# Bringing the first scale and shift in the order of the rows, ahead of a three-tile first projection

## The reference, cut to what matters

```python
def modulate(h, shift, scale):
    return h * (1 + scale) + shift

# trunk_layer, its beginning
sh1, sc1, gt1, sh2, sc2, gt2 = [m[:, None, :] for m in adaln_params(c, w_ada, b_ada)]   # silu(c) @ w_ada + b_ada, split in 6
shc1, scc1, gtc1, shc2, scc2, gtc2 = adaln_params(c_ctx, w_ada, b_ada)
h = modulate(rmsnorm(x, g1), sh1, sc1)
hc = modulate(rmsnorm(xc, g1), shc1, scc1)
z = h @ w_in                     # w_in: 1024 x 2304, here 18 tiles of 128 columns
```

## Time and profile before

| What | before |
|---|---|
| median of 3 runs | 2249.05 us (2247.86, 2249.05, 2258.78) |
| the profiled execution's own time | 2259.43 us |
| its span | 2257.6 us |
| mean granted TensorE clock | 0.978 |
| PE busy | 2152.4 us, 95% |
| DVE, ACT, POOL busy | 58%, 48%, 21% |
| DMA | 355.01 MB, mean 157 GB/s |

### The profile page before, as it was taken

One profiled execution on the slowest core, in us unless ns is written; L12 is line 12 of the kernel. 1 busy time (PEld: TensorE's weight loads), 2 busy tenths in 40 slices (PEclk: granted clock), 3 DMA queues, 4 the chain that ended last, 5 costly groups with the idle time before them and its releaser, 6 DMA issues.

```text
span 2257.6 us, 44527 instructions
## 1 busy us (share of the span) xinstructions
PE 2152.4 (95%) x19132; PEld 2028.1 (90%) x19132; DVE 1298.6 (58%) x2521; ACT 1088.5 (48%) x1880; POOL 479.4 (21%) x226
## 2 busy tenths in 40 slices
PE   4999999999999999998899998999999999999998
PEld 3977999999998789998778888999999999999998
DVE  2355454343344667565673456498388896666665
ACT  2443353232235446445442445555577776555554
POOL 0200100000002220001111342088856662000000
PEclk8999999999999999999899999999999999999999
DMA  7224333444444445764233325466544445555553
GB/s 282 76 103 150 127 117 134 162 154 168 169 160 144 139 165 183 243 205 137 98 131 113 131 85 187 140 208 186 187 131 143 149 148 173 186 187 187 186 187 129
DMA packets 97284, 355.01 MB, mean 157 GB/s; under 512 B 10688, under 2 KB 11712, under 8 KB 96704
## 3 DMA queue, kind: packets, MB, share of 16 engines
q1 hardware_dynamic: 97088, 352.18, 46.7%
HBM read 351.09 MB, written 1.05 MB: 156 GB/s over the span
## 4 chain that ended last, share of the span: by engine, by line
PE 85%; DVE 5%; ACT 3%; DMA 3%; issue 2%; POOL 2%; SPq 0%; ACTq 0%; DVEq 0%; POOLq 0%
PE ps L79 79%; PE ps L84 4%; DVE TL L114 2%; ACT TH L158 2%; PE ps L107 1%; DMA RAW<-in_wada 1%; POOL TL L114 1%; DMA RAW<-in_wdn 1%; ACT SQ L155 1%; DMA RAW<-in_wup 1%; POOL SM L114 0%; ACT Hh L158 0%; DVE ps L114 0%; DMA RAW<-in_win 0%; DVE SQ L114 0%
## 5 line engine op out<-in xcount | busy, mean ns | idle before, releaser
L158 ACT ACTIVATE TH<-RAW 128x1024 fp32r<-128x1024 f32 (+1 forms) x515 | 539.9, 1049 | 429.1 <-PE ps L79 197.9
L114 DVE TENSOR_TENSOR TL<-RAW,TH 128x1024 fp32r<-128x1024 f32 (+1 forms) x343 | 421.0, 1228 | 477.8 <-ACT TH L158 477.3
L114 POOL TENSOR_TENSOR TL<-RAW,TH 128x1024 fp32r<-128x1024 f32 x172 | 414.0, 2410 | 522.3 <-ACT TH L158 496.0
L79 PE MATMUL ps<-Hh,TL 128*128 128x256 f32 x1920 | 450.5, 287 | 24.5 <-ACT Hh L158 14.1
L79 PE MATMUL ps<-Hh,TH 128*128 128x256 f32 x1920 | 439.0, 281 | 0.0
L79 PE MATMUL ps<-Hl,TH 128*128 128x256 f32 x1920 | 438.0, 280 | 0.0
L79 PE MATMUL ps<-HXh,TL 128*128 128x256 f32 x1312 | 366.4, 283 | 5.7 <-POOL TL L114 2.6
L79 PEld LDWEIGHTS ps<-Hh,TL 128*128 128x128 f32 x1920 | 321.7, 191 | 53.4 <-issue 32.7
L79 PE MATMUL ps<-W,TH 128*128 128x256 f32 x2048 | 361.9, 281 | 0.0
L79 PE MATMUL ps<-HXh,TH 128*128 128x256 f32 x1312 | 360.7, 279 | 0.0
L79 PE MATMUL ps<-HXl,TH 128*128 128x256 f32 x1312 | 360.5, 279 | 0.0
(11 more groups left out here) (323 smaller groups left out, 3006.1 us busy)
## 6 DMA issues: line engine op xcount, KB each, us to landing
RAW<-in_wada SPq DMA_DIRECT2D x144, 512.0 KB, 3.6
RAW<-in_ut SPq DMA_DIRECT2D x128, 512.0 KB, 3.5
RAW<-in_v SPq DMA_DIRECT2D x128, 512.0 KB, 3.7
RAW<-in_wup SPq DMA_DIRECT2D x88, 512.0 KB, 4.3
RAW<-in_win SPq DMA_DIRECT2D x74, 512.0 KB, 4.4
RAW<-in_wdn SPq DMA_DIRECT2D x32, 512.0 KB, 4.4
RAW<-in_wout SPq DMA_DIRECT2D x24, 512.0 KB, 3.6
RAW<-in_wq SPq DMA_DIRECT2D x16, 512.0 KB, 3.5
```

The source lines that it names most:

```text
L79: return self.e.matmul(out, lhs, rhs, start=first, stop=last, skip_group_check=skip)
L114: return DRY if self.e is None else self.e.tensor_tensor(out, a, b, op)
L158: return DRY if self.e is None else self.e.activation(out, a, ACT.Copy, **kw)
```

## The change

What it does, in order of the program:

- Group 1 of w_ada now fetches the columns of group 2 and the other way round (`ADA_PLACE`), so that the first 8 tiles give shift and scale of rows 0 to 3, the next 8 those of rows 4 to 7.
- ("head", 0) has 6 tiles and ("head", 1) two; the other 8 are at ("side", 1) to ("side", 4), two each. In the list they lie behind w_in tiles 0, 1 and 2.
- DVE adds the squares of all 8 rows, so that `norm` on PE has 4 pieces instead of 16. `spread` follows ("head", 1). The lam products, their Exp and their four small DVE operations go to the very front.
- `scales` for this norm becomes `first_scales(0)`, after `columns(1)`, and `first_scales(1)`, after `columns(3)` in the middle of `norm_rows`. ACT makes rows 0 to 3, and before row 4 runs ("side", 1) to ("side", 4) and waits for the second half.
- w_in tile 0's low is made by DVE, tile 1's and 2's by POOL; ACT splits tiles 0 and 1 before the rows, tile 2 before row 2.
- `project_side` takes w_in tiles 0, 1 and 2. Rows 0 to 3 run on tiles 0 and 1, with two tiles of w_ada in front of each of rows 1, 2, 3 and 4; in front of row 4 also `columns(3)`, and then tile 2's rows 0 to 3. Row 4 runs on all three, rows 5 to 7 tile by tile.
- The constants go out in front of tile 24 instead of 18.

```diff
@@ weight_tiles
-            add(("wada", b, i), ins[f"wada{b}"][i], split=False)
+            add(("wada", b, i), ins[f"wada{b}"][4 * (ada_place(12 * b + i // 4) - 12 * b) + i % 4], split=False)
...
-        for i in WIN_FIRST[l]:
-            add(("win", l, i), win[i], pool=2)
+        for z, i in enumerate(WIN_FIRST[l]):
+            add(("win", l, i), win[i], pool=2 if l or z > 2 else min(z, 1))
+            if l == 0 and z == 2:
+                for k in range(1, 5):
+                    ada("side", k)
@@ _ada_plan
-    plan = [(("head", 0), 8), (("head", 1), 8)]
+    plan = [(("head", 0), 6), (("head", 1), 2)] + [(("side", k), 2) for k in range(1, 5)]
...
-ADA_TURNED = (3, 9, 35)
+ADA_TURNED = (1, 3, 9, 35)
+ADA_PLACE = {1: 2, 2: 1}
+def ada_place(g):
+    return ADA_PLACE.get(g, g)
@@ tensor_program, norm
-            pe.wait_ge(D if tag == ("n1", 0) else G, "sum", *tag, 4)
-            for k in range(4, 8):
-                if k > 4:
+            added = added_of(tag)
+            pe.wait_ge(D if tag == ("n1", 0) else G, "sum", *tag, added)
+            for k in range(added, 8):
+                if k > added:
                     pe.wait_ge(A, "square", *tag, k)
@@ project_side
             for n in range(together):
-                if n == 4 and midway:
-                    midway()
-                for z in range(len(tiles)):
+                if midway:
+                    midway(n)
+                if behind and n == behind:
+                    split_done(tiles[-1])
+                    for k in range(behind):
+                        row(len(tiles) - 1, k)
+                for z in range(len(tiles) - (n < behind)):
                     row(z, n)
@@ tensor_program, the head
-        ada("head", 0)
-        norm(("n1", 0), 512)
-        spread(("n1", 0), ROOT[0][:, 0:4], 1, D, "h_norm", "m1", 0, 7)
         for l in range(DEPTH):
             pe.wait_ge(D, "lp", l)
             o = bank(("lam", l), A, "le", l)
             pe.mm(o[:, 0:2], ones[0:32, :], nlam_lp[l][0:32, :], True, True).then_inc(*P.mark("lam", l))
+        ada("head", 0)
+        norm(("n1", 0), 512)
         ada("head", 1)
-        columns(3)
+        spread(("n1", 0), ROOT[0][:, 0:4], 1, D, "h_norm", "m1", 0, 7)
+        columns(1)
+        def side(n):
+            ada("side", n)
+            if n == 4:
+                columns(3)
...
-                project_side([("win", l, 0), ("win", l, 1)], h(T), T, h1, (A, "u", l, 0), (A, "u", l, 1))
-                for j in range(2):
-                    win(2 + j, T, A, "tr", l, "va", j)
+                project_side([("win", l, i) for i in range(3)], h(T), T, h1, (A, "u", l, 0), (A, "u", l, 1),
+                             (A, "tr", l, "va", 0), together=5, midway=side, behind=4)
+                win(3, T, A, "tr", l, "va", 1)
@@ add_squares
+    def added_of(tag):
+        return 7 if tag == ("n1", 0) else 4
-        for k in range(1, 5):
+        for k in range(1, added_of(tag) + 1):
@@ scalar_program
         def ada(*point):
-                if point[0] != "gap":
+                if point[0] != "gap" and g > 3:
                     highs(at_tile["wada", b, i] + AHEAD)
         def high_rows(tag, l, slot, shift, t, dst, streams):
-            act.wait_ge(D, "scale", *tag)
-            act.wait_ge(D, "ada", 12 * l + 2 * shift + 1)
+            if tag == ("m1", 0):
+                act.wait_ge(D, "scale", *tag, 0)
+            else:
+                act.wait_ge(D, "scale", *tag)
+                act.wait_ge(D, "ada", 12 * l + 2 * shift + 1)
             for k in range(8):
+                if tag == ("m1", 0) and k == 2:
+                    highs(at_tile["win", 0, 2])
+                if tag == ("m1", 0) and k == 4:
+                    for n in range(1, 5):
+                        ada("side", n)
+                    act.wait_ge(D, "scale", *tag, 1)
...
+        for l in range(DEPTH):
+            act.wait_ge(P, "lam", l)
+            act.act(nlam_le[l], ps("lam", l)[:, 0:2], ACT.Exp).then_inc(*A.mark("le", l))
         act.wait_sem("x_in", s_x, 16)
...
         ada("head", 1)
+        highs(at_tile["win", 0, 1])
@@ vector_program
         def ada(*point):
-                if point[0] != "gap":
+                if point[0] != "gap" and 12 * b + i // 4 > 3:
                     lows(at_tile["wada", b, i] + AHEAD)
+        def first_scales(half):
+            c = slice(8 * half, 8 * half + 8)
+            o = MOD[:, c].rearrange("p (m c) -> p m c", c=2)
+            src = ADAS[0][:, 16 + 8 * half:24 + 8 * half].rearrange("p (m c) -> p m c", c=2)
+            dve.wait_ge(D, "ada", 1 + 2 * half)
+            dve.ts(o, src, 1.0, 32.0, ALU.add, ALU.mult).then_inc(*D.mark("scale1", "m1", 0, half))
+            dve.wait_ge(D, "scale1", "m1", 0, half)
+            dve.tt(o, o, par("n1g0", 4 * half, 4 * half + 4).rearrange("p (m o) -> p m o", o=1).to_broadcast([128, 4, 2]),
+                   ALU.mult).then_inc(*D.mark("scale", "m1", 0, half))
@@ norm_rows, behind X times the spread of row k
+                if tag == ("m1", 0) and k == 6:
+                    for n in range(1, 5):
+                        ada("side", n)
+                    columns(3)
+                    first_scales(1)
@@ vector_program, the head
         ada("head", 1)
-        columns(3)
-        scales(("m1", 0), 0, "n1g0", 1, 0)
+        lows(at_tile["win", 0, 0])
+        columns(1)
+        first_scales(0)
@@ sync_program
-            if i == 18:
+            if i == 24:
                 sp.e.dma_start(CT[:, :], ins["cst"]).then_inc(s_cst, 16)
```

More of the change, by code:

```diff
@@ L664, in norm @@
                     c = slice(128 * tb, 128 * tb + 128)
-                    last = pe.mm(o[:, tb:tb + 1], (ACC if k == 4 else SQ[k % 3])[:, c], ones[:, 0:1],
-                                 k == 4 and tb == 0, k == 7, True)
+                    last = pe.mm(o[:, tb:tb + 1], (ACC if k == added else SQ[k % 3])[:, c], ones[:, 0:1],
+                                 k == added and tb == 0, k == 7, True)
             last.then_inc(*P.mark("ss", *tag))
@@ L693, in project, with project_side @@
             last.then_inc(*P.mark("used", i))
-        def project_side(keys, rhs, t, ready, *releases, ks=tuple(range(8)), together=8, midway=None):
+        def project_side(keys, rhs, t, ready, *releases, ks=tuple(range(8)), together=8, midway=None, behind=0):
             tiles = [at_tile[key] for key in keys]
@@ L700, in project_side @@
             for i, key, release in zip(tiles, keys, releases):
-                split_done(i)
+                if not behind or i != tiles[-1]:
+                    split_done(i)
                 o.append(bank(("z",) + key, *release))
@@ L891, in tensor_program @@
             project_side([("wout", l, 0), ("wout", l, 1)], mix, T, mix_ready, (D, "res1", l, 0), (D, "res1", l, 1),
-                         ks=MIX_ORDER, midway=lambda: head_spread(1))
+                         ks=MIX_ORDER, midway=lambda n: head_spread(1) if n == 4 else None)
             if l == 0:
@@ L1270, in square @@
             last.then_inc(*A.mark("square", *tag, k))
-            sq_read[j] = (D if tag == ("n1", 0) else G, "sum", *tag, max(k, 1)) if k < 5 else (P, "ss", *tag)
+            sq_read[j] = (D if tag == ("n1", 0) else G, "sum", *tag, max(k, 1)) if k <= added_of(tag) else (P, "ss", *tag)
         def high_rows(tag, l, slot, shift, t, dst, streams):
-            act.wait_ge(D, "scale", *tag)
-            act.wait_ge(D, "ada", 12 * l + 2 * shift + 1)
-            for k in range(8):
+            if tag == ("m1", 0):
[3 more added lines that the diff above has]
+                act.wait_ge(D, "ada", 12 * l + 2 * shift + 1)
+            for k in range(8):
+                if tag == ("m1", 0) and k == 2:
[4 more added lines that the diff above has]
+                    act.wait_ge(D, "scale", *tag, 1)
                 v = VT[k % 3]
@@ L1300, in scalar_program @@
         ada("head", 0)
-        for l in range(DEPTH):
-            act.wait_ge(P, "lam", l)
-            act.act(nlam_le[l], ps("lam", l)[:, 0:2], ACT.Exp).then_inc(*A.mark("le", l))
         ada("head", 1)
+        highs(at_tile["win", 0, 1])
         for l, y in enumerate(layers):
@@ L1372, in scalar_program @@
             else:
-                highs(at_tile["win", l, 1] + 1)
                 for j in range(2):
                     u_in(j)
+                    highs(later(("win", l, j), 3))
                 for j in range(2):
-                    highs(at_tile["win", l, 2 + j] + AHEAD)
+                    if j:
+                        highs(later(("win", l, 2), 3))
                     to_rows((l, "va", j), ("win", l, 2 + j), T, j, (D, "h_low", "m1", l, 6 + j))
@@ L1738, in columns @@
         def columns(g):
-            bias = par(["bada0", "bada1", "bada2"][g // 12], 4 * (g % 12), 4 * (g % 12) + 4)
+            c0 = 4 * (ada_place(g) % 12)
+            bias = par(["bada0", "bada1", "bada2"][g // 12], c0, c0 + 4)
             dve.wait_ge(P, "adac", g)
```

(18 more changed lines are left out.)

## The result

The changed kernel took 2230.02 us in the median of 4 runs (2227.03 to 2241.97), the kernel before, run beside it, 2253.91 (2247.86 to 2274.85): a ratio of 0.9884 with a 95% interval of 0.9836 to 0.9932. In two later comparisons, on two different chips and with 7 and 11 runs of the changed kernel, the ratio was 0.9922 (0.9885 to 0.9959) and 0.9926 (0.9900 to 0.9951). By the three ratios it is faster by 0.7 to 1.2%, 17 to 26 us; the forecast was 2232.

The account below looks back on a forecast made before the run. A long matmul stream behind a slow head: w_in 3's matmuls end at 67.4 instead of 84.65, so 17.2 us off the median 2249.05 gives 2231.8, rounded 2232; range 2223 to 2243, forecast's chance 0.66.

Parts of the forecast that it names:

- The moment that sets the gain: End of w_in 3's matmuls, 84.65 us before: forecast at 67.4, 17.2 us earlier, with the work after it unchanged.
- M: Start of ACT's copy behind the matmuls of w_in 3, 84.67 us in the kernel before.
- The start of the rows: Row 0 of Hh ready at 30.7 us instead of 52.1, 21.4 us earlier, with PE starting there at once.
- the two engines' meeting: DVE's first_scales(0) waits for POOL's low part of w_in 1, to 28.2 us; without the wait 26.2.
- The rival in which it slips in: DVE's small scale operations do not wait for POOL and the clock holds: 2225 to 2227 us, chance 0.13.
- The bank: PE's late start, 8.3 us after row 0, waits for spread's bank, which w_in tile 1 needs, free at 60.15.
- What is late next: SP's queue: w_ada 11 waits for POOL's low of w_in 2 (35.7), lands at 39.8; PE waits 2.3 us.
- The clock: PE at 1.2 GHz for some 4.7 us of dense rows, and low again some 4.5 us after the w_ada 11 wait.
- the last side tile: w_ada 15, last of the w_ada tiles among the rows: w_ada 14 and 15 forecast done at 49.2 us.
- The rivals with a clock low to the end of the stage, or beyond: 1.2 GHz to the end of w_in 2: 2243 us, chance 0.08; past w_in 3 and 12: slower, over 2260, chance 0.03.
- The rule on oscillation of the Trainium skill: Matmul pieces shorter than their transfer waits each start at the low clock; all of 30.7 to 67 could run low.
- The costs put at nothing: Lam work and three extra DVE sums hide under transfers (uncovered under 2 and 2.1 us); later constants have about 9 us slack.

## Why the prediction held, step by step

**The moment that sets the gain.** M was to move by 17.2 us and moved by 19.6; from there on the same operations of the two profiles stay 17 to 23 us apart up to the last stage. Taking everything after w_in 3 as unchanged fits this pair to 1.2 us; over all profiles it is known only to the scatter told above. That the sum (2232) lies so near the measured median (2230.02) is partly luck: the median of before used in it was 2249.05, single runs scatter more than the error of the sum, and in the two later comparisons the changed kernel's median was 2239.56 and 2245.97, the last outside the forecast's range, with the kernel before at 2255.71 and 2263.45 beside it.

**The start of the rows.** Forecast 30.7, measured 29.95; the 0.75 us lie ahead of the two engines' meeting, where POOL ended at 27.27 instead of 28.0. DVE's scale operation waited for POOL as the sum had it, 2.32 us. The rival in which it slips in was real as well: of the six profiles with w_in 1's low on POOL, four show 2.27 to 2.33 us and two 0.17. I had treated as a rule what is a race between a transfer and a bank copy, decided by tenths of a microsecond.

**The bank.** That PE's 8.3 us hung on spread's bank was read from the code against the profile's releaser, and the run with the lam work first showed it.

**What is late next.** SP's queue behind w_in 2's low: issue forecast at 35.7, measured at 35.02, and PE's wait 2.36 us for 2.3. The run with the early split confirmed it: with the split moved, the wait went. From issue to the start of its matmuls it took 3.67 us, for which I had taken 4.1.

**The clock.** Here the terms were too long. The windows of the changed kernel (span, busy PE, PEld, DVE, ACT, POOL, granted clock, DMA share, GB/s):

```profile
30.00:32.00 2.00, 1.91 (x9) 1.94 (x10) 1.73 (x3) 1.97 (x4) 0.00 (x0) 0.50 0.07 29
32.00:34.00 2.00, 2.00 (x37) 1.48 (x36) 1.00 (x2) 1.97 (x4) 1.39 (x1) 0.63 0.00 0
34.00:36.00 2.00, 2.00 (x32) 1.73 (x28) 1.75 (x2) 1.80 (x4) 0.99 (x1) 1.00 0.04 8
...
38.00:40.00 2.00, 1.31 (x22) 1.08 (x23) 0.00 (x0) 0.28 (x1) 0.00 (x0) 1.00 0.82 246
40.00:42.00 2.00, 2.00 (x22) 1.85 (x25) 0.17 (x1) 0.00 (x0) 0.00 (x0) 0.57 1.03 406
42.00:44.00 2.00, 2.00 (x32) 1.07 (x23) 0.00 (x0) 0.00 (x0) 0.00 (x0) 0.57 1.01 393
44.00:46.00 2.00, 2.00 (x43) 1.69 (x41) 0.00 (x0) 0.00 (x0) 0.00 (x0) 1.00 0.96 360
```

The clock was back at 2.4 GHz near 33.5, 3.4 us after the rows began, where I had counted 4.7, and the fall after PE's wait, at 40.3, lasted 3.4 us, not 4.5. The sum also ran low for longer than it said: with the clock back 4.5 us after 39.8, at 44.3, most of w_ada 12 and all of w_ada 13 and row 3 belong at the 2.4 GHz prices, some 1 us less than the 47.9 that it gives. These and the earlier start and landing bring the last side tile to 46.1 instead of 49.2. From there the working was close: 18.2 us to the end of w_in 3 forecast, 18.9 measured. The rivals with a clock low to the end of the stage, or beyond, are out: from 44 on it read 1.00.

Neither term is a constant of the kernel. In the other two profiles of the changed kernel the clock was back 3.8 and 4.5 us after PE began on the rows, and it did not fall at all behind the same wait (2.33 and 2.19 us). The second profile, 36 to 46:

```profile
36.00:46.00 10.00, 7.51 (x122) 6.05 (x110) 3.46 (x5) 2.19 (x5) 1.09 (x1) 1.00 0.78 270
```

The rule on oscillation of the Trainium skill (TensorE: Matmul & The Clock Gate, "HAM oscillation — how this bites in real kernels"), by which each piece behind a transfer wait starts at the low clock, is not borne out here: w_ada 11 took the 0.62 us of the high clock behind its wait in all three profiles, and the clock fell in one of them, 1.6 us later. That fall cost some 1.7 us, half of 3.4.

**The costs put at nothing.** The three more sums and the lam work cost nothing that shows. The constants had room at their new place: they were issued at 58.79, and PE's first product with them, at 77.2, follows without a wait for a transfer. What I had not seen is what their old place would have cost.

## What to carry to other kernels

Before an order is rearranged, ask of each long wait which instruction the code waits for, not which event came last: a ring of banks with an unlucky phase cost 6 us here and was cured by moving two tiny products. When work is moved out of a head, follow the in-order transfer queue: the next stall is at the first issue that waits for a late step of another engine. And compare kernels by a moment in the trace near the edit, measured from a moment just before it, when whole runs scatter by more than the edit is worth.

## What the runs showed of the hardware that was not expected

**Two speeds of one stage.** The last stage ran in 347.9 to 348.0 us in five profiles and in 361.5 to 361.6 in nine, with the granted clock at 1.00 both times. Two windows of 50 us inside it, of the kernel before, first and second profile:

```profile
1925.00:1975.00 50.00, 50.00 (x427) 50.00 (x426) 30.69 (x36) 28.38 (x35) 0.00 (x0) 1.00 0.59 185
```

```profile
1925.00:1975.00 50.00, 50.00 (x444) 50.00 (x443) 31.48 (x37) 29.99 (x38) 0.00 (x0) 1.00 0.61 193
```

427 or 444 matmuls in the same time, 117 or 113 ns from one to the next. Both kernels show both, and so do profiles taken on one chip, so neither the change nor the chip decides it alone. What does was not tried and stays open; it is 13.6 us, 0.6% of this kernel, and with the 13 us of the stretch before it, it makes up most of the scatter between these profiles.

**A small operation waits for a large one.** A DVE operation on 8 columns took 2.32 us because POOL had begun its 1024 columns 0.04 us before. The Trainium skill (GPSIMD Engine Reference, section "Specifications") says that POOL shares its SBUF interfaces with VectorE, for VectorE's operations with two SBUF inputs or in its two-port mode. The trace agrees that the two hold each other up: DVE's operation ended with POOL's (27.29 and 27.27), and took 0.17 us in every profile in which POOL was not running. It has one SBUF input; whether it ran in the two-port mode no run here shows.

**A clock column that starts late.** The granted clock reads 1.00 from the start of every profile to its first recorded fall, 17 to 41 us in, while the first three w_ada tiles take 1.03 or 1.04 us (once 1.00), the 1.2 GHz level, in all of them. In the kernel before the column is 1.00 up to 41.2, but w_ada tiles took 1.08 us up to 36.46 and 0.62 only at 39.14 and 40.38. Only after the first recorded fall can the column be believed; before it, the duration of a tile tells the clock.
